# Gated heads' queries and keys: upper and lower x in one matmul of 512 columns, halves summed by ScalarE and VectorE

## The reference, cut to what matters

```python
z = rms_norm(x, g_norm) @ w_in                       # (256, 1024) @ (1024, 8208)
qa, ka, va, ga, fa, qb, kb, vb, gb = jnp.split(z, cuts, axis=-1)
log_f = jax.nn.log_sigmoid(fa.astype(f32) + b_f.astype(f32))
ya = forgetting_attention(hA(qa), hA(ka), hA(va), log_f)   # heads of 64
```

## Time and profile before

| | |
|---|---|
| time, median of 3 runs | 770.98 us |
| the profiled execution: its time | 770.69 us |
| its span, first to last instruction | 768.9 us |
| TensorE busy | 760.5 us, 5026 matmuls |
| VectorE, ScalarE, GpSimd busy | 517.2, 409.8, 223.6 us |
| granted TensorE clock, mean | 0.999 |

### The profile page before, as it was taken

The page is one execution under the profiler, slowest core; times in us unless marked ns, Lnnn a source line. Parts: engine busy times, 40 slices in busy tenths (PEclk is TensorE's granted clock), DMA queues, the critical chain, the costliest instruction groups (busy, mean ns, idle before and its releaser), DMA issues.

```text
span 768.9 us, 12573 instructions
## 1 busy us (share of the span) xinstructions
PE 760.5 (99%) x5026; PEld 658.3 (86%) x5026; DVE 517.2 (67%) x779; ACT 409.8 (53%) x664; POOL 223.6 (29%) x176
## 2 busy tenths in 40 slices
PE   9999999999999999999999999999999999999997
PEld 8889987899877899987778888988888888888885
DVE  5876756665577558765567965778788676667553
ACT  6674458443696453353344554727857555456451
POOL 2110996730940000064029900126012111011010
PEclk9999999999999999999999999999999999999999
DMA  9999893588512746555435565430465556655751
GB/s 284 220 233 301 245 248 65 131 174 198 156 62 80 242 138 194 186 169 159 142 110 164 191 218 168 140 134 30 164 193 152 183 175 204 194 179 175 242 169 55
DMA packets 78490, 132.01 MB, mean 172 GB/s; under 512 B 4592, under 2 KB 28304, under 8 KB 78304
## 3 DMA queue, kind: packets, MB, share of 16 engines
q1 hardware_dynamic: 76928, 126.01, 55.7%
q0 software_dynamic: 1216, 5.09, 2.3%
q10 hardware_dynamic: 288, 0.11, 0.1%
HBM read 130.12 MB, written 1.06 MB: 171 GB/s over the span
## 4 chain that ended last, share of the span: by engine, by line
PE 97%; DVE 1%; ACT 1%; issue 0%; DVEq 0%; ACTq 0%
PE ps L1711 15%; PE ps L1715 15%; PE ps L1719 15%; PE ps L1769 10%; PE ps L1752 6%; PE ps L1756 6%; PE ps L1748 6%; PE ps L1777 5%; PE ps L1839 2%; PE ps L1855 2%; PE ps L1870 2%; PE ps L2225 1%; PE ps L2102 1%; PE ps L2054 1%; PE ps L2110 1%; PE ps L1799 1%
## 5 line engine op out<-in xcount | busy, mean ns | idle before, releaser
L1032 DVE TENSOR_TENSOR w_lo<-stage,w_hi 128x1024 fp32r<-128x1024 f32 x224 | 293.4, 1332 | 150.9 <-ACT w_hi L667 150.2
L667 ACT ACTIVATE w_hi<-stage 128x1024 fp32r<-128x1024 f32 x230 | 239.1, 1060 | 234.1 <-PE ps L1719 104.8
L1711 PE MATMUL ps<-w_hi,act_t 128*128 128x512 f32 (+1 forms) x368 | 100.5, 396 | 0.2 <-ACT act_t L694 0.2
L1719 PE MATMUL ps<-w_lo,act_t 128*128 128x512 f32 (+1 forms) x368 | 96.5, 385 | 0.0
L1769 PE MATMUL ps<-act_t,w_hi 128*128 128x512 f32 x352 | 84.1, 391 | 0.0
L1719 PEld LDWEIGHTS ps<-w_lo,act_t 128*128 128x128 f32 x368 | 68.1, 188 | 14.0
L1711 PEld LDWEIGHTS ps<-w_hi,act_t 128*128 128x128 f32 x368 | 66.5, 188 | 15.1 <-issue 2.5
L1715 PE MATMUL ps<-w_hi,act_t 128*128 128x512 f32 (+1 forms) x304 | 79.4, 384 | 0.0
L1769 PEld LDWEIGHTS ps<-act_t,w_hi 128*128 128x128 f32 x352 | 64.7, 188 | 12.6
L1715 PEld LDWEIGHTS ps<-w_hi,act_t 128*128 128x128 f32 x304 | 56.1, 188 | 11.6
L1748 PE MATMUL ps<-act_t,w_hi 128*128 128x256 f32 x416 | 58.8, 284 | 0.0
(11 more groups left out here) (384 smaller groups left out, 1153.1 us busy)
## 6 DMA issues: line engine op xcount, KB each, us to landing
stage<-in_even_w_in SPq DMA_DIRECT2D x62, 512.0 KB, 5.4
stage<-in_odd_w_in SPq DMA_DIRECT2D x48, 512.0 KB, 3.9
stage<-in_w_gate_up SPq DMA_DIRECT2D x44, 512.0 KB, 4.8
stage<-in_w_down SPq DMA_DIRECT2D x22, 512.0 KB, 4.7
stage<-in_even_w_out SPq DMA_DIRECT2D x16, 512.0 KB, 3.8
stage<-in_odd_w_out SPq DMA_DIRECT2D x16, 512.0 KB, 3.8
stage<-in_w_in SPq DMA_DIRECT2D x10, 512.0 KB, 3.7
stage<-in_w_out SPq DMA_DIRECT2D x8, 512.0 KB, 4.5
```

Source lines behind the costliest of these rows:

```text
L667: nc.scalar.activation(w_hi[:, u % RING, :], stage[:, u % RING, :], ACT.Copy).then_inc(hi_ready, 1)
L1032: nc.vector.tensor_tensor(w_lo[:, u % RING, :], stage[:, u % RING, :], w_hi[:, u % RING, :].bitcast(F32), ALU.subtract).then_inc(lo_ready, 1)
L1711: mm(out[:, b, :], a_hi(k)[:, tok[b]], hi[:, i, :], start=(k == 0), stop=False)
L1719: ins = mm(out[:, b, :], a_hi(k)[:, tok[b]], lo[:, i, :], start=False, stop=(k == k_tiles - 1))
```

## The change

qa and ka (four chunks, 16 units) get the form with side by side operands. A chunk now takes four banks, one for each group `m`: the left 256 columns hold upper x times upper weights plus upper x times lower weights, the right 256 hold lower x times upper weights. qa 0 and ka 0 are in banks 0 to 3, qa 1 and ka 1 in banks 4 to 7. TensorE waits for ga 1 to be drained before qa 0, and for `f_abs` (bank 4 read) before qa 1. ScalarE copies the right halves into `q0` or `k0` (two operations of 128 x 512), VectorE adds the left halves to them (two) and then multiplies by the row (two). qb and kb stay as they were.

```diff
+        WIDE = {("qa", 0): (0, 1, 2, 3), ("qa", 1): (4, 5, 6, 7), ("ka", 0): (0, 1, 2, 3), ("ka", 1): (4, 5, 6, 7)}
+        wide_names = list(WIDE)
+
+        def wide_parts(name, pair):
+
+            at = WIDE[name][2 * pair] * BANK
+            both = ps[:, at:at + 2 * BANK].rearrange("p (m v n) -> p m v n", m=2, v=2)
+            return both[:, :, 0, :], both[:, :, 1, :]
...
+            def take_lower(name, dst):
+
+                ahead(name)
+                chunk_done(act, name)
+                for pair in range(2):
+                    nc.scalar.activation(dst[pair], wide_parts(name, pair)[1], ACT.Copy).then_inc(lower_out, 1)
+
+            heads_of_chunk = lambda dst, c: [dst[:, 4 * c + 2 * pair:4 * c + 2 * pair + 2, :] for pair in range(2)]
+            for kind, dst in (("qa", q0), ("ka", k0)):
+                for c in range(2):
+                    take_lower((kind, c), heads_of_chunk(dst, c))
...
                 ahead((name, c))
+                if (name, c) in WIDE:
+                    out = [dst[:, 4 * c + 2 * pair:4 * c + 2 * pair + 2, :] for pair in range(2)]
+                    for pair in range(2):
+                        dve.wait_ge(lower_out, 2 * wide_names.index((name, c)) + pair + 1)
+                        TT(out[pair], wide_parts((name, c), pair)[0], out[pair], ALU.add).then_inc(parts_added, 1)
+                    for pair in range(2):
+                        dve.wait_ge(parts_added, 2 * wide_names.index((name, c)) + pair + 1)
+                        ins = TT(out[pair], out[pair], row[:].unsqueeze(1).to_broadcast([P, 2, S]), ALU.mult)
+                    ins.then_inc(drain_sem((name, c)), 1)
+                    return
                 chunk_done(dve, (name, c))
...
+            def wide_channels_unit(name, j, k_tiles, columns, there=always):
+
+                hi, lo = unit_of(name, j)
+                both = act_t[:, :, :].rearrange("p (v k) n -> p v k n", v=2)
+                ks = range(2 * j, 2 * j + 2)
+                for i, k in enumerate(ks):
+                    there[0](k)
+                    there[1](k)
+                    for m in range(4):
+                        mm(bank(WIDE[name][m]).rearrange("p (v n) -> p v n", v=2), columns(hi[:, i, :], m), both[:, :, k, :], start=(k == 0), stop=False,
+                           skip_group_check=True)
+                lower_there(name, j)
+                for i, k in enumerate(ks):
+                    for m in range(4):
+                        ins = mm(bank(WIDE[name][m], S), columns(lo[:, i, :], m), act_t[:, k, :], start=False, stop=(k == k_tiles - 1), skip_group_check=True)
+                ins.then_inc(unit_used, 1)
...
                 for j in range(chunks[name][1]):
-                    channels_unit(name, j, KD, columns, there)
+                    if name in WIDE:
+                        wide_channels_unit(name, j, KD, columns, there)
+                    else:
+                        channels_unit(name, j, KD, columns, there)
...
             ins.then_inc(f_done, 1)
+            chunk_drained(pe, ("ga", 1))
             channels(("qa", 0))
+            pe.wait_ge(f_abs, 1)
             channels(("qa", 1))
```

More of the change, by code:

```diff
@@ L293, in build @@
         wave_ready, wave_sin = sem("wave_ready"), sem("wave_sin")
+        lower_out, parts_added = sem("lower_out"), sem("parts_added")
         ret_scores, ret_decayed, ret_pv, ret_var, ret_scale, ret_centered, ret_out = (sem(n) for n in ("ret_scores", "ret_decayed", "ret_pv", "ret_var", "ret_scale", "ret_centered", "ret_out"))
```

## The result

The changed kernel takes 773.68 us (median of 6 runs, 772.43 to 774.61) against 770.95 us (770.47 to 771.45) in the same comparison: a ratio of 1.0033 with a 95% interval of 1.0022 to 1.0044. It is 2.7 us slower. The forecast was 769.4 us, with 768.8 to 771.2 as its range. The times also spread twice as wide as before. The profiled execution took 774.25 us, its span is 772.4 us.

A forecast was written before the change was run, and what follows sets the result against it. TensorE, busy 760.5 of 768.9 us, was taken as the bound. A gain of 1.55 us with no stalls gave a span of 767.35 us and a time of 769.4 us by the median, range 768.8 to 771.2.

The forecast's parts named there:

- The sum on TensorE: qa and ka, 16 units: eight 512-column matmuls replace sixteen of 256, 0.097 us a unit, 1.55 us gained.
- the prediction's lower end: qa and ka: each switch of matmul width costs extra, a unit takes 2.79 us, saving 1.4 us.
- The rival of 237 to 240 ns: Rival 2, qa and ka: a wide matmul costs nearly two narrow ones, gain 0 to 0.4 us, about 770.8 us; 4%.
- the gap rule: Trainium skill's warm matmul gap, N / 2.4 + 2.5 ns, which would make the TensorE gain only 0.3 us.
- The new waits for drained banks and for `f_abs`: TensorE before qa, ka and va chunks: drains and f_abs finish in time, cost nothing.
- ScalarE: Copies of 1.2 us a chunk ahead of the next upper weights: slack falls from 4.3 to 3.0 us, hidden.
- the failed step: VectorE drains of 2.5 to 3.9 us ahead of lower weights at ka 0 and ka 1: no stall taken.
- The loads: Loads start up to 2.7 us later, land in 5.4 us and start nearly four units, 11 us, ahead of use.
- the first named the mechanism: Rival 1: VectorE late for lower weights, multiplies 1.31 us beside GpSimd, stalls 0.3 and 0.8 us, 770.5 us; 16%.
- The third: Rival 3: VectorE's adds slowed beside GpSimd too, 5.1 us of stalls, +3.5 us, 774.5 us; 6%.

The follow-up runs named there:

- the spread later: Changed kernel with GpSimd issuing the 2 MB spread of forget terms only once TensorE has used unit 20: 772.93 us, ratio 1.0023 to the kernel before.
- the wide matmuls alone: Changed kernel without copies and adds, drained by two multiplies, lower x times upper weights left out of queries and keys: 769.80 us, ratio 0.9983 to the kernel before.
- the sum in PSUM: Changed kernel with the adds writing back to PSUM and the multiplies reading PSUM: 770.10 us, ratio 0.9986 to the kernel before.

## Why the prediction was wrong

- *The sum on TensorE*: right in kind, 1.55 us forecast, 1.36 and 1.37 measured. A wide matmul has a pitch of (57.16 - 55.33) / 8 = 229 to 230 ns, not 228. The gain is that of the prediction's lower end, the one that charges each switch of width. The rival of 237 to 240 ns, and the gap rule beside it, are out.
- *The new waits for drained banks and for `f_abs`*: cost nothing, as forecast; none stands in the waits.
- *ScalarE*: the copies took 0.54 us each and delayed nothing that TensorE waited for directly. But the step ended at va; the units queued ahead of the exponentials were not followed, and there the late loads cost 1.0 us.
- *VectorE*: **the failed step**: "I take no stall: the middle of both ranges has slack". TensorE stood still for 4.0 us instead: 2.0 at unit 27, 1.0 at unit 31, 1.0 at the attention. The multiply was bounded at 0.69 to 1.31 us; on average it took 1.07 to 1.19 beside GpSimd, within these bounds but near the upper one in all three pairs, though single ones took up to 1.78. The adds were right, at 0.64. A row of two operands in SBUF beside GpSimd was at hand, and I weighed it down by the one operation in four that had run free.
- *The place*: the chain was followed at ka 0 and ka 1 only. "GpSimd works from 76.57 us on" was written next to it, and the drain of qa 1 falls right there, with line 1227 (0.42 us before, 1.51 as line 1258) behind it; both were left out. The first and longest stall came from them together with the late unit 26: either alone left unit 27 in time (the profiles of the spread later and of the wide matmuls alone).
- *The loads*: the slack was read from one execution's landings. Unit 26's load stood 1.5 us ahead of a 2 MB transfer; with the change it fell behind it and came 4 us later.
- *The rivals*: the first named the mechanism and priced it at 1.1 us of stalls, for 770.5 us; it was 4.0 us in the profile. Its 0.8 us at unit 35 came out as priced once the loads were in order (the spread later), but not its 0.3 at unit 31, and the 1.3 us at the attention were not in it. The third, the only one on the slower side, put its price on the wrong operation: the adds were not slowed. With 8% on slower, the text had the right cause and the wrong odds.

The contention is told first by the rows: lower weights 1.2 us alone and up to 2.37 beside GpSimd, the multiplies 0.64 and 1.15 on average. The Trainium skill ("GPSIMD Engine Reference", Key points) names the two cases that contend, VectorE instructions with two SBUF inputs and those in a 2-port mode. The runs agree with the first: with one of two inputs in PSUM the operation kept 0.64 us. Line 1258 has one SBUF input and still went from 0.42 to 1.51 us; that is not the first case, and no row shows the mode in which it ran, so the second is not shown here.

## What to carry to other kernels

When a change lengthens a step on an engine that makes the bound engine's operands, follow that engine's queue from the first place where the step occurs, at the slow price of every operation in it, also of those that the change doesn't touch; where one engine is busy 99% of the time, the others can be late only by as much as the buffers between them hold. Keep one operand of a VectorE operation in PSUM where GpSimd works at the same time: here it turned a loss of 2.7 us into a gain of 1.0. And read slack in loads as what one order of issues gave: a load that one profile has 1.5 us ahead of a large transfer can be behind it in the next kernel.

## What the runs showed of the hardware

- With both tensors in SBUF a 128x512 operation of VectorE took 0.64 us alone and, beside GpSimd, 1.07 to 1.53 us as the mean of a pair (nine pairs in three profiles); with one in PSUM 0.64 us either way, also with the result written to PSUM.
- In the changed kernel the slowing fell on one of each pair: 0.67 us for the first multiply, 1.54 to 1.78 for the second, which ended 0.55 to 0.56 us after GpSimd's operation did.
- A `tensor_scalar` of 128x512 within SBUF took 0.42 us alone; beside GpSimd it took 1.14 to 1.52 us in five profiles and 0.41 to 0.42 in two (the sum in PSUM, the wide matmuls alone).
- A 512 KB load issued 0.14 us behind a 2 MB one was ready for ScalarE after 11.9 us, against at most 8.2 when it was issued 1.5 us ahead of it.
- A TensorE stream of 512-column matmuls has a pitch of 227 ns in long rows and 230 ns where every eight alternate with eight of 256 columns (120 ns).
